# Modulation slabs multiplied two at a place, at every other place among the attention units

## The chip, the cores and the metric

One core of a Trainium2 chip runs the whole program. Its engines have instruction streams of their own and meet only at semaphores: PE (matrix multiply, with its weight loads as PEld), DVE (vector), ACT (activation), POOL and SP, which here issues the weight transfers. The metric is the device time of one execution in microseconds (us), lower is better.

## The reference, cut to what matters

Two blocks on 256 tokens of width 1024 in float32. The first is an attention of two kinds and a convolved feed-forward. The second has two layers; each layer needs six modulation vectors for the latents and six for the context, made of one conditioning vector each:

```python
c_act = jax.nn.silu(c)
cc_act = jax.nn.silu(c_ctx)
for l in range(DEPTH_2):
    ...
    mod_l = [m[:, None, :] for m in jnp.split(c_act @ ada_w[l] + ada_b[l], N_MOD, axis=-1)]
    mod_c = jnp.split(cc_act @ ada_w[l] + ada_b[l], N_MOD, axis=-1)
    ...
    h_l = modulate(xl, norm_mix_g[l], mod_l[0], mod_l[1])
    ...
    xl = xl + mod_l[5] * sq_relu_mlp(modulate(xl, norm_mlp_g[l], mod_l[3], mod_l[4]), w_mlp1[l], w_mlp2[l])
```

The matrices `ada_w` are 1024 x 6144 for each layer, 48 MB together. Their products have two rows each, and nothing needs them before the norm of the layer that they belong to.

## The kernel before, in words

All weights pass through a ring of four slots of 1 MB (`ring`, `SLOTS = 4`). SP issues slab after slab in the order in which they are used, and waits before each until the slab four places earlier in the order has been used up (`freed`). A modulation slab is 256 rows by 1024 columns of `ada_w`; there are 48, loaded by `load_mods` (the transfer is line 471). Multiplying one is `mod_rows_of`: eight float32 products of `cact` (two columns, padded to 32) with 256 columns, in four column groups of the array, into PSUM bank 4 or 5, which ends in a count on `mod_ready` (its rows in the profile are line 658). Four slabs in a row (n = 4d to 4d + 3) add up to one eighth of the twelve vectors of a layer; after the fourth, `copy_mods` on DVE (lines 2056 to 2066) transposes the bank and copies two columns of it to `mod_in`.

These slabs are put among the attention units, where PE's work comes in small pieces. There are three attention stages: that of block 1 (16 units, line 953 on, the first eight of kind A, the others of kind B), that of layer 0 of block 2 (32 units) and that of layer 1 (16 units). They get 12, 24 and 12 slabs. In layer 0 units alternate between long ones (latent queries, 512 keys) and short ones (context queries, 256 keys); in layer 1 all are long. Place u of the loop is what PE does in its turn u, in this order:

- the scores of unit u + 2 (`scores1`, line 916; `scores2`, line 1025), which need the exponentials of unit u done, since they use its PSUM banks
- the turn of unit u (`turn_weights`, line 929): PE transposes the weights of unit u. It waits for `a_ready` of unit u, except in units of kind A
- the outputs of unit u - 1 (`outputs1`, line 942; `outputs2`, line 1037)
- the modulation slab of this place, if it has one

DVE goes in its own order through turns of its own: the maximum of unit v (line 2331, in block 1 lines 2189 and 2193), the scaled output of unit v - 3 (`out2`, line 2352; `out1`, line 2219), the weights of unit v - 1 (`weights2`: reciprocal 2339, a small product 2342 and the combination 2346, which counts `a_ready`; `weights1`: 2208), and then `copy_mods` for the place v - 2. The output of unit v - 3 can be scaled only when PE's outputs of it are done, and the weights of unit v - 1 come behind it. In block 1 DVE also normalises two key heads in its turns 3 and 5 (`norm_head`, reciprocal at line 2171). ACT makes the exponentials (line 1619, 1464) and copies the turned weights out of PSUM (line 1473).

Which places have a slab is set by `spread(units, first, count)`: slab n of a stage goes to place n * units // count. With 12 slabs on 16 places and 24 on 32 this is every place except 3, 7, 11 and so on. After an attention stage of block 2 come the product with the narrow dt weights (line 765), the scaling of the outputs (line 2377) and the turns at line 845; `fill` (line 779) issues products whose result nobody uses.

Of the kernel before, what the change touches and what calls it, by code (L numbers as in the profile page):

```python
# [119 lines left out]
def two_blocks(nc, a, const, out):  # L120
    with ExitStack() as ctx:
# [41 lines left out]
        at = 9 * P  # L163
# [219 lines left out]
        at = 9 * P  # L383
# [36 lines left out]
        def spread(units, first, count):  # L420

            at = {}
            for n in range(count):
                at[n * units // count] = first + n
            return at

        mods_of = [spread(len(UNITS1), 0, EARLY), spread(len(units2(0)), EARLY, LATE + EARLY),
# [4 lines left out]
        def _(sp):  # L432
# [17 lines left out]
            mods = [0]  # L450
# [13 lines left out]
            def load_mods(n):  # L464

                for _ in range(n):
                    s = len(done) % SLOTS
                    freed(len(done))
                    l, j = divmod(mods[0], N_MOD // 2)
                    j, kk = divmod(j, 4)  # L470
                    sp.dma_start(slot(s, 2, D), of_layer("ada_w_2", l)[:, 2 * kk:2 * kk + 2, j * D:(j + 1) * D])\
                        .then_inc(slot_loaded[s], 16)
                    mods[0] += 1
                    booked((mod_ready, mods[0]))
# [40 lines left out]
            slabs(1, KT, 128, lambda j: w_in[:, :, 640:768], lambda j: 2 * j)  # L515
            sp.dma_start(K[:, 3 * P:], const[:, 3 * P:]).then_inc(tables_loaded, 16)
            wide(w_in, 768, 6)
            load_mods(len(mods_of[0]))
            wide(w_out, 0, 4)
            for j in range(FFT):  # L520
                up_slabs.append(len(done))
# [13 lines left out]
            for l in range(LAYERS):  # L535
                wi = of_layer("w_in_2", l)
                first_slab["q", l] = len(done)
                wide(wi, 0, 4)
                wide(wi, 1024, 4)
                wide(wi, 2048, 4, per=TT)  # L540
                wide(wi, C_GA, 4)
                load_mods(len(mods_of[1 + l]))
                slabs(1, KT, 64, lambda j: wi[:, :, C_DT:C_DT + 64], lambda j: TT * j)
                first_slab["attn_o", l] = len(done)
                wide(of_layer("w_attn_o_2", l), 0, 4)

                nz = len(y_chunks(l)) // 2
                per_group = 4 + nz
                after = [1, 2, 4, per_group]

                def group_parts(s, q, g):
                    half = slot(s, KT, P)
                    full = slot(s, KT, 256)
                    if q < 2:
                        return [(half, wi[:, :, bass.ds(g * GW + (C_X + q * P), P)])]
                    if q == 2:
                        return [(full[:, :, 0:P], wi[:, :, bass.ds(g * P + C_B, P)]),
                                (full[:, :, P:2 * P], wi[:, :, bass.ds(g * P + C_C, P)])]
                    return [(full, wi[:, :, bass.ds(g * GW + C_Z, GW)])]

                s0 = len(done)
                first_slab["ssd", l] = s0
                for q in range(4):
                    load(lambda s: group_parts(s, q, 0), after[q])
                with sp.Fori(1, GROUPS) as g:
                    for q in range(4):
                        s = (s0 + q) % SLOTS

                        sp.wait_ge(tile_ready, g * per_group + (total[0] + after[q] - per_group))
                        for dst, src in group_parts(s, q, g):  # L570
                            sp.dma_start(dst, src).then_inc(slot_loaded[s], 16)
                for g in range(1, GROUPS):
                    for q, n in enumerate(after):
                        booked((tile_ready, total[0] + per_group * g + n), 2 if q == 2 else 1)
                total[0] += per_group * GROUPS
                first_slab["gs", l] = len(done)
                for j in range(KT):
                    load(lambda s: [(slot(s, KT, P), wi[:, :, C_GS + j * P:C_GS + (j + 1) * P])], 1)
                    total[0] += 1
                first_slab["ssd_o", l] = len(done)  # L580
                wo = of_layer("w_ssd_o_2", l)
                slabs(KT, YT, P, lambda j: wo[:, :, bass.ds(j * P, P)], lambda j: j)
                wide(of_layer("w_out_2", l), 0, 4)
                w1, w2 = of_layer("w_mlp1_2", l), of_layer("w_mlp2_2", l)
                first_slab["mlp", l] = len(done)
                if l == 0:
                    for half in range(2):
                        wide(w1, half * HID // 2, HIDT // 4)
                        slabs(KT, YT, P, lambda j: w2[:, YT * half:YT * (half + 1), bass.ds(j * P, P)], lambda j: j)
                else:  # L590
                    wide(w1, 0, HIDT // 2)
                    for n in range(KT):
                        for half in range(2):
                            load(lambda s: [(slot(s, YT, P), w2[:, YT * half:YT * (half + 1), n * P:(n + 1) * P])], 1)
                        total[0] += 1
# [11 lines left out]
        def _(pe):  # L607
# [41 lines left out]
            def mod_rows_of(n):  # L649

                w = slot(weights(), 2, D).rearrange("p k (t g q) -> p k t g q", g=4, q=32)
                done, kk = divmod(n, 4)
                if kk == 0 and done > 1:
                    pe.wait_ge(mod_copied, done - 1)
                for k in range(2):
                    for g in range(4):
                        rows_of = PS[32 * g:32 * g + 32, 4 + done % 2, 0:256].rearrange("p (t q) -> p t q", q=32)
                        mm = pe.matmul(rows_of, cact[:, 2 * kk + k, :], w[:, k, :, g, :], start=(kk == 0 and k == 0),  # L658
                                       stop=(kk == 3 and k == 1))
                mm.then_inc(*c.made(mod_ready))  # L660
# [291 lines left out]
            for u in range(n_u + 1):  # L952
                if u + 2 < n_u:
                    scores1(u + 2)
                if u < n_u:
                    turn_weights(u, 4, prob[:, u % 2, 0:T] if UNITS1[u][0] == "A" else None)
                if u >= 1:
                    outputs1(u - 1)
                if u in mods_of[0]:
                    mod_rows_of(mods_of[0][u])  # L960
            c.skip(p_ready, 2)
            pe.wait_ge(*c.need(tok_scaled, LT))
            bank4[0] = 0
# [27 lines left out]
            for l in range(LAYERS):  # L991
# [24 lines left out]
                units = units2(l)  # L1016
# [25 lines left out]
                mods = mods_of[1 + l]  # L1042
# [3 lines left out]
                for u in range(n_u + 1):  # L1046
                    if u + 2 < n_u:
                        scores2(u + 2)
                    if u < n_u:
                        turn_weights(u, TT if units[u][1] < LT else LT)  # L1050
                    if u >= 1:
                        outputs2(u - 1)
                    if u in mods:
                        mod_rows_of(mods[u])
                c.skip(p_ready, 4)
                pe.wait_ge(*c.need(o_done))
                ring_begin(dve_freed)
# [909 lines left out]
        def _(dve):  # L1967
# [88 lines left out]
            def copy_mods(n):  # L2056

                done, kk = divmod(n, 4)
                dve.wait_ge(*c.need(mod_ready))
                if kk == 3:  # L2060
                    m0 = 8 * (done % (N_MOD // 8))
                    turned_rows = mod_rows[:, done % 2, :]
                    dve.transpose(turned_rows, PS[:, 4 + done % 2, 0:256]).then_inc(*c.made(mod_copied))
                    settle(mod_copied)
                    dve.tensor_copy(mod_in[:, m0:m0 + 8, :], turned_rows.rearrange("p (t q) -> p t q", q=32)[:, :, 0:2])\
                        .then_inc(*c.made(mod_read))
# [52 lines left out]
            for b in range(V_TURNS):  # L2119
                n = min(512, n_rows - 512 * b)  # L2120
# [112 lines left out]
            for u in range(n_u + 3):  # L2233
                if u < n_u:
                    max1(u)
                if u >= 3:
                    out1(u - 3)
                if u == n_u + 1:
                    scale_half(0)
                if 1 <= u <= n_u:  # L2240
                    weights1(u - 1)
                    settle()
                    settle(a_ready)
                if u in (3, 5):
                    norm_head(12 + (u - 3) // 2)
                if u - 2 in mods_of[0]:
                    copy_mods(mods_of[0][u - 2])
            settle(mod_read)
            c.skip(t_ready, 2)
            scale_half(1)  # L2250
# [44 lines left out]
            for l in range(LAYERS):  # L2295
# [60 lines left out]
                for u in range(n_u + 3):  # L2356
                    if u < n_u:
                        max2(u)
                    if u >= 3:
                        out2(u - 3)  # L2360
                    if 1 <= u <= n_u:
                        weights2(u - 1)
                    if u - 2 in mods:
                        copy_mods(mods[u - 2])
                c.skip(t_ready, 2)
                settle(mod_read)
                dve.wait_ge(*c.need(tok_rms))
# [532 lines left out]
```

## Time and profile before

| what | us |
|---|---|
| median of 3 runs | 2565.73 (2563.46 to 2565.87) |
| span of the profiled execution | 2566.1 |
| PE busy | 2489.1 (97%) |
| DVE, ACT, POOL busy | 1224.1, 1125.6, 1494.5 |

The span of the profile is 0.4 us above the median of the runs, and it carries no other time of its own, so what is worked out on the trace can be added to the median as it is. PE is busy for 97% of the span, the others for half of it or little more. A busy share is an average over stages, so it does not say what a change in one stage costs; for that the windows and timelines of the stage are read.

### The profile page before, as it was taken

Reading aid. Unit: us, or ns where it says so; the run is one execution under the profiler, and the core shown is the slowest. Engines: PE = TensorE matmul, PEld = TensorE weight load, DVE = VectorE, ACT = ScalarE, POOL = GpSimd, SP = SyncE. Lnnn points to the kernel's source line nnn. Section 1 sums busy time; section 2 is a strip of 40 time slices with the busy share of each in tenths; the row PEclk is TensorE's granted clock in tenths of the full one; section 3 lists DMA queues with packets and bytes.
Section 4 is the critical chain, followed back from the end, with each engine's and each line's share of the span. In section 5 each row is a group of like instructions: output and inputs, shape, how many; then the busy total and the mean of one; then the engine's idle time right before and its main releaser. Section 6 shows DMA issues by size and latency. Waiting matters only on the chain.

```text
span 2566.1 us, 39740 instructions
## 1 busy us (share of the span) xinstructions
PE 2489.1 (97%) x15548; PEld 2170.1 (85%) x15548; DVE 1224.1 (48%) x2583; ACT 1125.6 (44%) x2371; POOL 1494.5 (58%) x1318
## 2 busy tenths in 40 slices
PE   8999999999899999999999999999989999999999
PEld 7779997885688888888888888888859888889998
DVE  3545502236747888874243112121366888844210
ACT  2345533115526776774022002042364766654532
POOL 1019775870354554543975888864324666577976
PEclk9999999999999999999999999999999999999999
DMA  7566463237532222214322333332454233364564
GB/s 211 182 191 185 128 165 103 83 96 260 191 99 67 75 58 66 74 50 156 98 82 88 95 98 99 99 113 85 150 183 115 71 95 90 83 171 156 186 169 116
DMA packets 388969, 313.03 MB, mean 122 GB/s; under 512 B 12576, under 2 KB 374082, under 8 KB 387778
## 3 DMA queue, kind: packets, MB, share of 16 engines
q1 hardware_dynamic: 385874, 297.75, 39.2%
q10 hardware_dynamic: 2352, 12.59, 1.3%
q8 instruction: 109, 1.79, 0.3%
q0 software_dynamic: 576, 0.43, 0.2%
q14 instruction: 58, 0.48, 0.1%
HBM read 303.40 MB, written 7.34 MB: 121 GB/s over the span
## 4 chain that ended last, share of the span: by engine, by line
PE 73%; POOL 10%; DVE 7%; issue 5%; DMA 2%; ACT 2%; POOLq 1%; SPq 0%; DVEq 0%; ACTq 0%
PE PS L707 35%; PE PS L1109 10%; POOL rounded L2702 10%; PE PS L765 5%; PE PS L1116 4%; PE PS L730 2%; DVE mid_a L2445 2%; PE PS L1150 2%; PE PS L1237 2%; PE PS L658 2%; PE PS L1159 2%; PE PS L1037 1%; PE PS L929 1%; PE PS L1025 1%; PE PS L1171 1%
## 5 line engine op out<-in xcount | busy, mean ns | idle before, releaser
L2702 POOL TENSOR_TENSOR rounded<-ring,rounded 128x512 fp32r<-128x512 f32 (+1 forms) x872 | 1113.6, 1310 | 729.7 <-ACT rounded L1376 417.7
L707 PE MATMUL PS<-rounded 128*128 128x256 f32 (+1 forms) x6864 | 1135.4, 327 | 6.7 <-POOL rounded L2702 3.3
L707 PEld LDWEIGHTS PS<-rounded 128*128 128x128 f32 x6864 | 1016.6, 190 | 119.3 <-POOL rounded L2702 4.1
L2725 POOL TENSOR_TENSOR rounded<-ring,constants 128x512 fp32r<-128x512 f32 x216 | 229.3, 1092 | 248.2 <-PE PS L707 125.2
L1109 PE MATMUL PS<-rounded 128*128 128x512 f32 (+1 forms) x1536 | 343.5, 380 | 5.8 <-DVE mid_a L2445 5.1
L1109 PEld LDWEIGHTS PS<-rounded 128*128 128x128 f32 x1536 | 275.3, 188 | 61.2 <-DVE mid_a L2445 3.7
L1376 ACT ACTIVATE rounded<-ring 128x2048 fp32r<-128x2048 f32 (+1 forms) x99 | 180.0, 1822 | 136.6 <-DMA ring<-in_w_mlp_dram 55.1
L2445 DVE SCALAR_TENSOR_TENSOR mid_a<-PS,V,mid_a 128x510 f32<-128x510 f32 (+3 forms) x256 | 182.2, 714 | 25.5 <-ACT mid_a L1705 18.0
L1743 ACT ACTIVATE rounded<-constants,big 128x128 fp32r<-128x128 f32 x384 | 149.8, 390 | 0.0
L1743 ACT ACTIVATE rounded<-constants,mid_v 128x128 fp32r<-128x128 f32 x384 | 149.8, 390 | 0.0
L1116 PE MATMUL PS<-rounded 128*128 128x256 f32 x1152 | 147.8, 286 | 0.0
L1116 PEld LDWEIGHTS PS<-rounded 128*128 128x128 f32 x1152 | 142.6, 191 | 1.8
L1920 ACT ACTIVATE PS<-PS 128x512 f32<-128x512 f32 (+1 forms) x64 | 30.4, 475 | 251.7 <-DVE PS L2633 251.6
L2610 DVE SCALAR_TENSOR_TENSOR xT<-PS,mod,xT 128x256 f32<-128x256 f32 x40 | 17.9, 481 | 244.4 <-PE PS L707 244.4
L2633 DVE TENSOR_SCALAR PS<-PS 128x512 f32<-128x512 f32 (+1 forms) x64 | 36.1, 566 | 188.1 <-PE PS L707 177.8
L2482 DVE SCALAR_TENSOR_TENSOR big<-big,by_head 128x128 f32<-128x128 f32 x192 | 108.1, 621 | 18.9 <-POOL big L2803 18.6
L1659 ACT ACTIVATE rounded<-ring 128x1024 fp32r<-128x1024 f32 (+1 forms) x64 | 93.1, 1476 | 30.1 <-DMA ring<-in_w_in_dram 30.1
L765 PE MATMUL PS<-rounded 128*128 128x256 f32 x768 | 102.7, 290 | 0.0
L2318 DVE TENSOR_TENSOR edec<-PS,constants 128x256 f32<-128x256 f32 x32 | 13.6, 425 | 180.4 <-PE PS L1009 180.1
L765 PEld LDWEIGHTS PS<-rounded 128*128 128x128 f32 x768 | 96.3, 191 | 1.8
L2331 DVE TENSOR_REDUCE stat<-PS 128x2 f32<-128x1024 f32 (+1 forms) x48 | 50.0, 1045 | 81.0 <-PE PS L1025 80.8
L730 PE MATMUL PS<-rounded 128*128 128x256 f32 (+1 forms) x480 | 86.2, 339 | 1.4 <-DVE rounded L2623 0.9
(263 smaller groups left out, 3134.2 us busy)
## 6 DMA issues: line engine op xcount, KB each, us to landing
ring<-in_w_mlp_dram SPq DMA_DIRECT2D x64, 1024.0 KB, 5.5
ring<-in_w_in_dram SPq DMA_DIRECT2D x56, 1024.0 KB, 5.4
ring<-in_ada_w_dram SPq DMA_DIRECT2D x48, 1024.0 KB, 5.2
ring<-in_w_in_dram SPq DMA_DIRECT2D x81, 512.0 KB, 4.1
ring<-in_w_up_dram SPq DMA_DIRECT2D x44, 512.0 KB, 5.1
ring<-in_w_ssd_o_dram SPq DMA_DIRECT2D x16, 1024.0 KB, 5.9
ring<-in_w_out_dram SPq DMA_DIRECT2D x12, 1024.0 KB, 5.1
ring<-in_w_down_dram SPq DMA_DIRECT2D x16, 704.0 KB, 5.0
```

Of the source, the lines that this page charges most:

```text
L707: mm = pe.matmul(PS[:, b, 0:cols], w[:, k, m * P:(m + 1) * P], x(half * kt + k), start=(half == 0 and k == 0 and n_pass == 0), stop=(half ...
L730: mm = pe.matmul(PS[:, b, 0:cols], w[:, k, m % 2 * P:(m % 2 + 1) * P], x(k), start=(k == 0 and n_pass == 0), stop=(k == kt - 1 and n_pass ...
L765: mm = pe.matmul(PS[:, b, 0:width], x[:, k, t * P:(t + 1) * P], w[:, k, :], start=(k == 0 and n_pass == 0), stop=(k == KT - 1 and n_pass = ...
L1109: mm = pe.matmul(PS[:, b, 0:cols], w[:, k, m:m + P], x[:, k, 0:cols], start=(k == 0 and x is hs_hi and w is w_hi), stop=(k == KT - 1 and w ...
L1116: mm = pe.matmul(PS[:, b, t * GW:(t + 1) * GW], x[:, k, t0:t0 + P], w[:, k, :], start=(k == 0 and x is hs_hi and w is w_hi), stop=(k == KT ...
L1376: act.activation(view(R, at[n % len(at)], size), ring[:, slab % SLOTS, 0:size], ACT.Copy)\
L1659: act.activation(view(R, group_hi(s, q), words), ring[:, s, 0:words], ACT.Copy).then_inc(*c.made(round_ready))
L1743: act.activation(seg_parts[d][n][:, r * P:(r + 1) * P], mask, ACT.Copy, scale=dta_parts[n][:, t, h:h + 1]).then_inc(*c.made(seg_in))
L2445: ins = dve.scalar_tensor_tensor(out=cv[:, :, to], in0=u[:, :, fr], scalar=V[:, bass.ds(g * st + (cw + 32 * (d + 2) + off), 1)], in1=cv[:, ...
L2482: step(dve.scalar_tensor_tensor(out=m, in0=cb_lo[:, t, :], scalar=dt[:, t, g * GH + r:g * GH + r + 1], in1=m, op0=ALU.mult, op1=ALU.add))
L2702: ins = pool.tensor_tensor(lo[:, r], raw[:, r], hi[:, r], ALU.subtract)
L2725: ins = pool.tensor_tensor(hi[:, r], raw[:, r], ones[:, 0:1].broadcast_to([P, 512]), ALU.mult)
```

## The change

`spread` hands out two slabs at a time: for even n, slabs n and n + 1 both go to place n * units // count. Twelve slabs on 16 places now lie at places 0, 2, 5, 8, 10 and 13, two at each; 24 on 32 places lie at 0, 2, 5, 8, 10, 13, 16, 18, 21, 24, 26 and 29. PE multiplies the two behind each other, DVE takes both in the turn that belongs to the place. The same slabs are loaded in the same order.

```diff
         def spread(units, first, count):
 
             at = {}
-            for n in range(count):
-                at[n * units // count] = first + n
+            for n in range(0, count, 2):
+                at[n * units // count] = (first + n, first + n + 1)
             return at
...
-            load_mods(len(mods_of[0]))
+            load_mods(sum(map(len, mods_of[0].values())))
...
-                load_mods(len(mods_of[1 + l]))
+                load_mods(sum(map(len, mods_of[1 + l].values())))
...
-                if u in mods_of[0]:
-                    mod_rows_of(mods_of[0][u])
+                for n in mods_of[0].get(u, ()):
+                    mod_rows_of(n)
...
-                    if u in mods:
-                        mod_rows_of(mods[u])
+                    for n in mods.get(u, ()):
+                        mod_rows_of(n)
...
-                if u - 2 in mods_of[0]:
-                    copy_mods(mods_of[0][u - 2])
+                for n in mods_of[0].get(u - 2, ()):
+                    copy_mods(n)
...
-                    if u - 2 in mods:
-                        copy_mods(mods[u - 2])
+                    for n in mods.get(u - 2, ()):
+                        copy_mods(n)
```

## Rows read from the trace of the kernel before

**Rows 1.** Page, chain by engine; stages by window: us, busy PE, PEld, DVE, ACT, POOL, clock, DMA.

```profile
PE 73%; POOL 10%; DVE 7%; issue 5%; DMA 2%; ACT 2%; POOLq 1%; SPq 0%; DVEq 0%; ACTq 0%
...
96.00:147.00 51.00, 47.14 (x451) 32.21 (x449) 35.78 (x111) 31.22 (x91) 0.00 (x0) 0.97 0.77 257
585.00:682.00 97.00, 90.48 (x809) 54.00 (x809) 72.62 (x172) 61.66 (x225) 0.28 (x1) 1.00 0.83 281
1848.00:1907.00 59.00, 54.72 (x454) 32.75 (x454) 42.95 (x86) 36.21 (x111) 0.00 (x0) 1.00 0.74 233
```

**Rows 2.** Timeline of PE, layer 0, places 2 to 4: start, us, line, [idle before].

```profile
596.88 1.07 PE L658 MATMUL PS<-ring,cact 128*32 128x256 f32 x16
597.88 0.70 PE L1025 MATMUL PS<-big 64*128 64x256 f32 x4
598.51 0.44 PE L929 MATMUL PS<-constants,big 128*128 128x128 f32 x2
598.79 1.06 PE L1037 MATMUL PS<-mid_v,big 128*128 128x128 f32 x8
599.77 1.13 PE L1025 MATMUL PS<-big 64*128 64x512 f32 x4
601.40 0.66 PE L929 MATMUL PS<-constants,big 128*128 128x128 f32 x4 [0.50 <-DVE big L2346]
```

**Rows 3.** Timeline of DVE beside it.

```profile
596.03 1.23 DVE L2331 TENSOR_REDUCE stat<-PS 128x2 f32<-128x1024 f32 x1 [0.68 <-PE PS L1025]
597.17 0.34 DVE L2352 TENSOR_SCALAR mid_o<-PS,stat 128x128 f32<-128x128 f32 x1
...
597.88 0.48 DVE L2346 SCALAR_TENSOR_TENSOR big<-big,stat 128x256 f32<-128x256 f32 x1
...
599.88 0.35 DVE L2352 TENSOR_SCALAR mid_o<-PS,stat 128x128 f32<-128x128 f32 x1 [0.49 <-PE PS L1037]
...
600.34 0.22 DVE L2342 SCALAR_TENSOR_TENSOR stat<-stat,neg_lam 128x1 f32<-128x1 f32 x1
600.60 0.75 DVE L2346 SCALAR_TENSOR_TENSOR big<-big,stat 128x512 f32<-128x512 f32 x1
```

**Rows 4.** Waits of PE for DVE, layer 0, layer 1, block 1: total us, times, longest.

```profile
PE PS L929 <- DVE big L2346: 4.4, 9, 0.6
...
PE PS L929 <- DVE big L2346: 2.7, 5, 0.6
...
PE PS L929 <- DVE big L2208: 1.5, 4, 0.6
```

**Rows 5.** Timeline of PE, the last turns of layer 0 and of layer 1.

```profile
676.23 0.66 PE L929 MATMUL PS<-constants,big 128*128 128x128 f32 x4 [0.56 <-DVE big L2346]
...
678.70 0.44 PE L929 MATMUL PS<-constants,big 128*128 128x128 f32 x2 [0.36 <-DVE big L2346]
...
1903.69 0.66 PE L929 MATMUL PS<-constants,big 128*128 128x128 f32 x4 [0.63 <-DVE big L2346]
```

**Rows 6.** Timeline of block 1: two turns of kind A, two of kind B; DVE's reciprocal of a head.

```profile
109.95 0.66 PE L929 MATMUL PS<-constants,big 128*128 128x128 f32 x4
111.95 1.75 DVE L2171 RECIPROCAL big<-big 128x256 f32<-128x256 f32 x1
112.01 0.66 PE L929 MATMUL PS<-constants,big 128*128 128x128 f32 x4
...
121.19 0.66 PE L929 MATMUL PS<-constants,big 128*128 128x128 f32 x4
123.82 0.66 PE L929 MATMUL PS<-constants,big 128*128 128x128 f32 x4 [0.50 <-DVE big L2208]
```

**Rows 7.** Line 471, the transfers of the modulation slabs.

```profile
DMA to landing us min/median/max: 4.9/5.2/10.2
```

**Rows 8.** Windows after and at the end of layer 0's attention (columns as in rows 1).

```profile
676.00:682.00 6.00, 4.42 (x41) 3.30 (x41) 2.54 (x9) 2.69 (x12) 0.28 (x1) 1.00 1.07 350
690.00:694.00 4.00, 0.50 (x3) 0.51 (x4) 3.97 (x6) 0.00 (x0) 4.00 (x3) 0.56 0.80 262
```

## The prediction, made before the change was run

> **What bounds the kernel now.** I read the chain of work that ended last first, then windows over the three attention stages, then the timelines of PE and DVE inside them, and the waits of PE last. The chain runs on PE for 73% of the span, and in the three stages that the change touches PE is busy for 47.14 of 51, 90.48 of 97 and 54.72 of 59 us [rows 1]. So these stages go at PE's pace: what PE does there, and each wait of PE there, lengthens the kernel one for one. The reader is to see in the timeline of PE that pieces follow each other without a gap where a place has a slab, and that the one gap of 0.50 us stands in the turn that follows the place without one [rows 2]. The waits of PE for DVE's weights come to 4.4 us in 9 waits in layer 0, 2.7 in 5 in layer 1, 1.5 in 4 in block 1 [rows 4]: 8.6 us in all, and these are what a slab can hide.
>
> **Why a place without a slab (a bare place) costs.** Take the turn of unit 4 in layer 0. PE ends the outputs of unit 2 at about 599.77 and goes on to the scores of unit 6, which start then. Only after those outputs can DVE scale them (599.88), and the weights of unit 4 come behind that in DVE's order: a reciprocal, a small product at 600.34, the combination from 600.60 for 0.75 us; PE's turn starts at 601.40 [rows 2, 3]. That chain is 601.40 - 599.77 = 1.63 us long. PE has the scores of a long unit to put beside it, 1.13 us, so 1.63 - 1.13 = 0.50 us is left, which is the wait in the row. A slab between outputs and scores takes 597.88 - 596.88 = 1.00 us [rows 2], and 1.00 + 1.13 is more than 1.63: nothing is left. A second slab at the same place takes 1.00 us more and hides nothing, because nothing is left to hide. Nor does it put DVE ahead: three places with slabs in a row leave 0.5 us of slack each, and the wait after them is still the whole 0.50.
>
> For a short unit the last link is 0.48 us instead of 0.75 [rows 3], so the chain is 1.63 - 0.27 = 1.36 us, and the scores above it, of a short unit too, take 598.51 - 597.88 = 0.63 us [rows 2]: a bare place costs 0.73 us. Where the maximum of a long unit is in DVE's way, the scaling is later: at 597.17 it starts 0.29 us after PE went on at 596.88, behind a maximum that ran from 596.03, instead of 599.88 - 599.77 = 0.11 [rows 2, 3]. That is 0.18 us more, 0.90. No row of before shows a bare place ahead of a short unit, so these two are bounded. Unit 31 is short and waited 0.36 with a slab's 1.07 over it [rows 2, 5], so with only 0.63 over it the wait can't be under 0.36; and with nothing over it, it is the whole chain, 1.36 to 1.43. I take 0.73 and 0.90, which are nearest to the links of the chain as rows show them.
>
> **Layer 0** (32 units, pairs at 0, 2, 5, 8, 10, 13, 16, 18, 21, 24, 26, 29). Bare places were 8, and are 20. The turns behind them: 11 of long units (2, 4, 8, 10, 12, 16, 18, 20, 24, 26, 28) at 0.50, 5.5 us; short units 5, 13, 21, 29 at 0.73, 2.9 us; short units 7, 15, 23, behind a long unit's maximum, at 0.90, 2.7 us; and unit 31, ahead of which no scores are left, at 1.36 (before it had a slab's 1.00 over it and waited 0.36 [rows 5]), 1.4 us. Sum 12.5 us. Before it was 4.4 [rows 4]. Change +8.1 us.
>
> **Layer 1** (16 long units, pairs at 0, 2, 5, 8, 10, 13). Turns 2, 4, 5, 7, 8, 10, 12, 13 at 0.50 are 4.0 us, turn 15 has neither scores nor slab above it and waits the 1.63 (before 0.63 with a slab [rows 5]). Sum 5.6 against 2.7 [rows 4], change +2.9 us.
>
> **Block 1** (16 units, same places). In kind A PE does not wait for DVE's weights: turn 3 to turn 4, over the bare place 3, takes 112.01 - 109.95 = 2.06 us with no wait [rows 6]. Bare places in the first half are free, but for one: the reciprocal of a key head occupies DVE from 111.95 for 1.75 us [rows 6], the scaling of the outputs of unit 3 comes after it and after the maximum of unit 6, and PE's outputs of unit 4 need that. Place 4, now bare, no longer covers it: I work out 0.45 us. In kind B a bare place costs 0.50 (121.19 to 123.82 is 2.63 us with that wait in it [rows 6]); turns 8, 10, 12, 13 are 2.0 us, turn 15 without scores and slab 0.50 + 0.63 = 1.1. Sum 3.1 against 1.5 [rows 4]: +1.6, and with the 0.45, +2.1 us.
>
> **The rest of the edit.** PE's products, DVE's copies and ACT's work are the same in number and size: nothing. After a fourth slab DVE transposes and copies (some 0.6 us) in the turn of the pair, beside PE's bare place instead of beside a slab. In the order of DVE this lies between the weights of one unit and the maximum of the next; it can make a turn behind a bare place late by 0 to 0.4 us, at most once for each of the 12 copies (an estimate: DVE's own work for a unit of kind B fills the 2.6 us between turns behind a bare place, so little of the copy is covered). To see whether such things add up I laid the durations of the rows end to end in the order of the three engines, each step at the later of its own engine and of what it needs. For before this puts the turn of unit 31 of layer 0 77.1 us behind that of unit 4; in the trace it is 678.70 - 601.40 = 77.3 [rows 2, 5]. For the new places it gives +8.1, +3.1 and +2.4 us, 13.5 in all, against 8.1 + 2.9 + 2.1 = 13.1 by hand. I take 13.3.
>
> **Transfers.** The order of the slabs is kept. SP issues a slab when the slab four before it has been used, so a pair is replaced by the pair after next, at least five places later: by the laid-out durations its second slab is wanted 13.3 us after its slot came free. Landing takes 5.2 us in the median and 10.2 at most [rows 7]; two behind each other at the median are 10.4. That is under 13.3, so loads cost nothing; were this cover gone, PE would wait for the second slab of a pair. The slabs of attn_o and w_out behind the modulation slabs are issued at the same place or a place sooner, and no wait of PE behind the stages is for them.
>
> **What the stage's end covers.** Behind each stage PE waits for DVE's scaling, which starts when the last unit is done; nothing there was early. So none of the 13.3 us is given back.
>
> **Forecast.** 2565.7 + 13.3 = 2579.0 us.
>
> **Rivals.**
> *Faster: the pair banks its lead.* If DVE and ACT could use the second slab's 1.00 us to get ahead, a pair would cover the two bare places behind it (slack of 0.5 + 1.0 against 2 x 0.50) and all the waits would go: 2565.7 - 8.6 = 2557.1. It decides from the point where the weights of a unit are ready a whole place before their turn. For it: the buffers are two deep. Against it: the weights of unit u stand in DVE's order behind the scaled output of unit u - 2, which PE makes one place before; and slack did not save up over three slab places [rows 2]. Chance 0.03.
> *No change: half of it is banked.* If the bare place next to a pair were free and only the second in a row paid, there would be 4 + 8 + 4 = 16 paying places of about 0.5 us, 8 us against 8.6: 2565.1. The same row speaks against it. Chance 0.04.
> *Much slower: the second slab of a pair is late.* If in layer 0, where demand is highest (281 GB/s [rows 1]), both transfers of a pair took the longest landing, one behind the other, 20.4 us would go by from the issue of the first, which is 1.0 us ahead of the second; the second is wanted 14.7 us after its slot came free, by the laid-out durations. That is 20.4 - 1.0 - 14.7 = 4.7 us late, for each of the 10 pairs that are reloaded: 2579.0 + 47 = 2626. Against it: the median is half of that, and line 658 waits for nothing in the trace. Chance 0.03.
> *Slower: the clock falls.* In a window of 4 us in which PE is busy for 0.50 the granted clock is 0.56, that is near 1.2 GHz instead of 2.4; in the window 676 to 682, where it is busy for 4.42 of 6.00, it kept 1.00 [rows 8]. Should short waits in a row bring it down, the work of the second bare place, 2.06 us, would double at each of the 16 pairs of bare places: +33, 2612. Chance 0.04. The Trainium skill (TensorE: Matmul & The Clock Gate, section "A second HAM failure mode: psum-queue depth-cycling") says that a kernel whose PE pauses briefly and often between groups of products can swing between half and full clock; that speaks against this change, and by it the time would be nearer to this rival. The trace does not agree with it so far: the last six microseconds of layer 0's attention are idle for 1.58 us in short waits and show 1.00 [rows 8].
>
> **How the numbers follow.** The forecast has 0.86. Its own range, low end: long turns at 0.40 and short ones at 0.36, the least that rows allow [rows 5], no copy in the way and no 0.45 give 11 x 0.40 + 7 x 0.36 + 1.4 - 4.4 = +3.9, 8 x 0.40 + 1.6 - 2.7 = +2.1 and 4 x 0.40 + 1.1 - 1.5 = +1.2, 7.2 in all, 2573. High end: long turns at 0.63, the longest wait behind a long unit [rows 5], short ones at 0.90 give +10.2, +3.9 and +2.6, and the copies in half of their places 6 x 0.4 = 2.4, 19.1 in all, 2585. The range 2573 to 2585 leaves 0.14 to the rivals and needs no widening. About 0.2% (5.1 us) is what a measurement of this kernel can tell from no change. Faster by more than that: the first rival, 0.03. Within: the second, 0.04. Slower: 0.93.
>
> **What would show it.** The windows of the three stages should grow from 51, 97 and 59 us to about 53, 105 and 62; the waits of PE's turn for DVE from 4.4, 2.7 and 1.5 us to about 12.5, 5.6 and 3.1, in about 20, 9 and 5 waits; slabs should still take 1.00 us each and wait for nothing; outside the stages nothing should move by more than 0.5 us. A wait in front of line 658 would mean the third rival, a granted clock under 1.00 inside layer 0 the fourth, waits of 0.50 behind only every other bare place the second. The prediction would be wrong if PE's waits stayed near 8.6 us, or if something behind a stage had been waiting for its slabs all along.

## Result: 9 to 11 us slower

| | before | changed |
|---|---|---|
| median of 6 runs each | 2565.57 us (2563.46 to 2567.08) | 2575.02 us (2571.47 to 2580.92) |
| ratio to before, 95% interval | | 1.0038 [1.0028, 1.0048] |
| the profiled execution | 2565.9 us | 2580.92 us, its span 2579.1 us |
| predicted | | 2579.0 us (2573 to 2585) |

The change costs 9.45 us. Timed once more beside the experiments it cost 11.1 us (ratio 1.0046 [1.0032, 1.0060]); that is e10 below. Forecast were 13.3 us: inside the range, and 20 to 40% more than the two measurements.

The profile after. First the chain by engine and the three stages in windows (us, busy PE, PEld, DVE, ACT, POOL, granted clock, DMA share, GB/s), which answer to [rows 1]; the windows were chosen for this trace, from the stage's first work to just behind its last:

```profile
PE 68%; POOL 10%; DVE 8%; issue 5%; DMA 1%; ACT 1%; POOLq 1%; SPq 0%; DVEq 0%; ACTq 0%
...
96.00:150.00 54.00, 48.58 (x456) 34.76 (x452) 35.17 (x110) 31.37 (x94) 0.00 (x0) 0.93 0.74 254
588.00:692.00 104.00, 89.52 (x809) 55.23 (x809) 72.41 (x172) 61.64 (x225) 0.26 (x1) 1.00 0.74 263
1859.00:1920.00 61.00, 54.18 (x454) 33.38 (x454) 42.70 (x85) 35.87 (x111) 0.00 (x0) 1.00 0.66 227
```

The stages are 3, 7 and 2 us longer, with the same records on PE (456 for 451, 809, 454), and PE is busy in them for slightly less than before in two of the three. What was added is idle time of PE. Whose it is, the waits of PE say (engine, line waited at, releaser: us, times, longest), for layer 0, layer 1 and the two places of block 1, as in [rows 4]:

```profile
PE PS L929 <- DVE big L2346: 12.1, 19, 1.3
...
PE PS L929 <- DVE big L2346: 5.6, 9, 1.6
...
PE PS L929 <- DVE big L2208: 3.1, 5, 1.1
...
PE PS L942 <- DVE mid_o L2219: 0.9, 2, 0.6
```

Forecast were 12.5 us in about 20 waits, 5.6 in 9, 3.1 in 5, and 0.45 at the outputs of unit 4 of block 1. The timeline of PE shows each kind at its place, beside the pair of slabs (start, duration, line, [idle before]):

```profile
600.62 1.93 PE L658 MATMUL PS<-ring,cact 128*32 128x256 f32 x32
602.48 0.70 PE L1025 MATMUL PS<-big 64*128 64x256 f32 x4
603.12 0.44 PE L929 MATMUL PS<-constants,big 128*128 128x128 f32 x2
603.39 1.06 PE L1037 MATMUL PS<-mid_v,big 128*128 128x128 f32 x8
604.38 1.13 PE L1025 MATMUL PS<-big 64*128 64x512 f32 x4
606.01 0.66 PE L929 MATMUL PS<-constants,big 128*128 128x128 f32 x4 [0.50 <-DVE big L2346]
606.50 0.61 PE L1037 MATMUL PS<-mid_v,big 128*128 128x128 f32 x4
607.04 0.70 PE L1025 MATMUL PS<-big 64*128 64x256 f32 x4
608.40 0.44 PE L929 MATMUL PS<-constants,big 128*128 128x128 f32 x2 [0.66 <-DVE big L2346]
...
615.18 0.44 PE L929 MATMUL PS<-constants,big 128*128 128x128 f32 x2 [0.86 <-DVE big L2346]
...
688.72 0.44 PE L929 MATMUL PS<-constants,big 128*128 128x128 f32 x2 [1.29 <-DVE big L2346]
```

Behind the pair at place 2 the turn comes without a wait. Then come the two bare places 3 and 4: behind the first the long unit's turn waits 0.50 us (forecast 0.50), behind the second the short one's 0.66 (0.73). A short turn behind a long unit's maximum waits 0.86 (0.90), unit 31 waits 1.29 (1.36). And the first row holds what was missed: the pair takes 602.48 - 600.62 = 1.86 us, not twice the 1.00 of [rows 2].

To compare stages below I take the time from the first turn (line 929) to the product with the dt weights (line 765) in the layers, and to the first turn at line 845 in block 1. Before: 91.39 us in layer 0, 53.78 in layer 1 and 46.88 in block 1; this last has a stretch with a granted clock of 0.58 in it (see e4), so for block 1 the measure of before is e2, which has its placement and no such stretch inside the stage.

### The profile page after: what moved, and what is told of

Read it like the earlier page. It is cut to its first block, busy times and chain, and to the rows that moved or that the text cites. A ratio compares the mean times of both kernels' runs of the same rounds, so it can differ in the third digit from the quotient of the medians.

```text
span 2579.1 us, 39731 instructions
## 1 busy us (share of the span) xinstructions
PE 2490.9 (97%) x15548; PEld 2176.5 (84%) x15548; DVE 1218.1 (47%) x2583; ACT 1125.6 (44%) x2371; POOL 1494.4 (58%) x1318
## 4 chain that ended last, share of the span: by engine, by line
PE 68%; POOL 10%; DVE 8%; issue 5%; DMA 1%; ACT 1%; POOLq 1%; SPq 0%; DVEq 0%; ACTq 0%
PE PS L707 32%; PE PS L1109 10%; POOL rounded L2702 10%; PE PS L765 4%; PE PS L1116 4%; PE PS L730 2%; DVE mid_a L2445 2%; PE PS L1150 2%; PE PS L1237 2%; PE PS L658 2%; PE PS L1159 2%; PE PS L1037 1%; PE PS L929 1%; PE PS L1171 1%; DVE mid_v L2499 1%
```

## Experiments

Each experiment is compared with runs of the kernel before made beside it. Their medians are 2564.67 us for e1 to e4, 2565.30 for e5 to e8 and 2564.91 for e9 and e10.

**e1 and e2: one stage's share at a time.** `spread` gets the number of slabs a place as an argument; e1 pairs them in block 1 alone, e2 in the two layers alone.

```diff
-        def spread(units, first, count):
+        def spread(units, first, count, step):
...
-            for n in range(0, count, 2):
-                at[n * units // count] = (first + n, first + n + 1)
+            for n in range(0, count, step):
+                at[n * units // count] = tuple(range(first + n, first + n + step))
```

e1 calls it with 2, 1, 1 for the three stages, e2 with 1, 2, 2.

> Two slabs at a place in block 1 only; layers 0 and 1 keep one slab at a place, as before. Theory (each bare place costs the wait that a slab hid, a pair of slabs in one piece costs 1.86 us instead of 2 x 1.00): waits of PE's turn for DVE's weights in block 1 go from 1.5 to about 3.1 us, one wait of 0.35 to 0.45 for the scaled output, six pairs give back 6 x 0.14 = 0.8 us: +1.3 us against before, with the granted clock at 1.00 to the end of the stage. Clock theory: the 1.07 us wait in front of the last turn, which was 0.17 before, lets the clock fall to half at 146 us as in the profile of the changed kernel; then the end of the stage and the first product of w_out take 2 to 3 us more, +3 to +5 against before. Rival (nothing in block 1 matters since behind it is slack): 0.

> Two slabs at a place in layers 0 and 1 only; block 1 as before. Theory: layer 0 +6.4 to +6.7 us, layer 1 +2.1 to +2.3 us as the sum of waits (12.1 against 4.4, 5.6 against 2.7) less 0.14 us for each of 18 pairs: +8.5 to +9 us against before, and no spread between runs beyond that of before, since the clock is at 1.00 in both stages. If the clock fall behind block 1 is what spread the runs of the changed kernel, this one has none of it. Rival (the layers' waits are covered by slack behind the stages): under +4.

e1: 2565.83 us, ratio 1.0010 [1.0001, 1.0019], +1.2 us. e2: 2574.99 us, ratio 1.0040 [1.0026, 1.0054], +10.3 us. The layers' share is somewhat above the 8.5 to 9 expected. Together 11.5, against 9.45 and 11.1 for the whole change: the stages add up, and no paying back of one in another is seen. The stages themselves: block 1 47.00 us in e1 against 45.45 in e2, layer 0 91.38 in e1 against 98.17 in e2, layer 1 53.77 against 56.12. That is +1.55, +6.8 and +2.35, 10.7 us.

**e3: is it the work or the cover?** At each bare place of layers 0 and 1 the changed kernel also multiplies one idle product, of about 0.5 us, into the modulation bank that is not in use; its result is never read.

```diff
+            def idle_products(next_slab, k):
...
+                for _ in range(k):
+                    pe.matmul(PS[:, 4 + done % 2, 256:512], ones, K[:, 0:SEQ], start=True, stop=True)
...
+                    if u not in mods and u < n_u:
+                        idle_products(done_mods, 1)
```

> The changed kernel, with one product whose result nobody uses (128 x 256, about 0.5 us of PE) put at each of the 30 bare places of layers 0 and 1. Theory (PE waits there anyway for the chain outputs, scaled output, weights, turn): the product takes the place of the wait; the waits of the turn for DVE fall from 12.1 and 5.6 us by about 0.5 each, and the time stays that of the changed kernel within 2 us. Rival (PE's own work is what the places cost): 30 x 0.5 = +15 us against the changed kernel, about 2590.

The two layers last 98.13 and 56.13 us, as without the 30 products (98.15 and 56.12 in e10); the kernel takes 2577.27 us, ratio 1.0060 [1.0044, 1.0076], in four runs. That is 12.6 us over before, where the changed kernel was 9.45 and 11.1 over it and the rival wanted some 25. Waits and timeline of PE in layer 0 (line 670 is the product; PE's other lines have moved by 10, DVE's by 13):

```profile
597.53 0.60 PE L670 MATMUL PS<-constants 128*128 128x256 f32 x2
598.05 1.13 PE L1035 MATMUL PS<-big 64*128 64x512 f32 x4
599.25 0.66 PE L939 MATMUL PS<-constants,big 128*128 128x128 f32 x4
...
601.64 0.44 PE L939 MATMUL PS<-constants,big 128*128 128x128 f32 x2 [0.23 <-DVE big L2359]
```

```profile
PE PS L939 <- DVE big L2359: 3.2, 9, 0.9
```

The long turn has no wait left, the short one 0.23 instead of 0.66: the waits fall from 12.1 to 3.2 us and the stage keeps its length. A bare place has about half a microsecond free, and the turn's time is set by DVE's chain, not by PE's work. A pair's second slab lies outside that gap, behind the turn that has nothing left to hide.

**e4: does the clock fall at the end of block 1 because of the change?** In the profiled execution of the changed kernel the granted clock drops there. Windows as above:

```profile
144.00:148.00 4.00, 3.08 (x20) 2.98 (x21) 1.70 (x7) 2.08 (x6) 0.00 (x0) 0.77 1.10 361
148.00:152.00 4.00, 2.99 (x15) 2.59 (x15) 1.34 (x4) 2.69 (x8) 0.00 (x0) 0.50 0.14 43
```

0.50 is 1.2 GHz. At the beginning of this stretch PE had waited 1.07 us for the turn of unit 15 (144.34). e4 is the changed kernel with two idle products in each of the last two places of block 1:

```diff
+                if n_u - 2 <= u < n_u:
+                    idle_products(EARLY, 2)
```

> The changed kernel, with two products whose result nobody uses at each of the last two bare places of block 1 (14 and 15), about 1.0 us each, where PE waited 1.07 and 0.57 us. Theory (the idle end of block 1's attention lets the granted clock fall to half, from about 146 to 156 us, in some executions): the clock stays at 1.00 there, the stretch from the last turn to the second product group of w_out is 2 to 3 us shorter than in the profile of the changed kernel, and the runs spread less, at about 2573. Rival (the clock falls for the window's own phase whatever PE does there): it falls here too, and the time is that of the changed kernel.

e4: 2575.73 us (about 2573 expected), ratio 1.0044 [1.0031, 1.0056], clock 1.00 in both windows, block 1 47.11 us. But the changed kernel itself, profiled once more (e10), has 1.00 there too, at 47.01 us, and so has e1; and e2, whose block 1 is that of before, fell (so did e5 below). Windows of e2 and then of e10:

```profile
144.00:148.00 4.00, 2.20 (x17) 1.97 (x17) 1.75 (x6) 2.65 (x9) 0.00 (x0) 0.90 0.58 185
148.00:152.00 4.00, 4.00 (x17) 3.58 (x16) 0.00 (x0) 1.75 (x4) 0.00 (x0) 0.67 0.02 4
```

```profile
144.00:148.00 4.00, 2.81 (x24) 2.46 (x23) 1.54 (x5) 2.40 (x7) 0.00 (x0) 1.00 0.88 288
148.00:152.00 4.00, 2.82 (x17) 2.62 (x18) 1.05 (x3) 2.96 (x8) 0.00 (x0) 1.00 0.03 6
```

So this fall goes with the execution and not with the placement, as far as one profile each can tell; it does not explain the 10 us. The start of block 1 varies in the same way (granted clock from 100 to 104: 0.58 before, 0.78 in the changed kernel, 1.00 in e1, e2, e4 and e10). The profiled pair of executions differs by 13.0 us of span, which looks like the forecast of 13.3, but by luck: against e10 the first profile of the changed kernel loses some 3.5 us between the last turn of block 1 and the second group of products with the weights behind it, where its clock fell, and not every execution has this. What makes an execution fall stays open.

**e5: four slabs at every fourth slab's place.** The same as e1 with 4, 4, 4.

> Four slabs at a place, at every fourth slab's place (0, 5, 10 on 16 places; 0, 5, 10, 16, 21, 26 on 32). Theory by the laid-out durations (each place without a slab costs its wait, a piece of k slabs costs 0.14 + 0.86 k us): block 1 +3.2, layer 0 +10.4, layer 1 +4.6, +18 us against before, if the four slabs are in the ring when PE comes to them. Four transfers of 1 MB have five places, some 13 to 15 us, from the slot coming free to use: at 2.7 us each behind each other and 5.2 to land they just fit. Transfer rival: PE waits in front of the slabs (line 658), 1 to 5 us at each of the nine groups that are reloaded, +10 to +40 more. Rival (a bare place costs nothing if another bare one precedes it): waits stay near those of pairs, +12.

2590.07 us, ratio 1.0098 [1.0082, 1.0113], +24.8 where 18 were expected. Timeline and waits of PE in layer 0, and the landing of the slabs' transfers (line 471, us):

```profile
599.53 2.80 PE L658 MATMUL PS<-ring,cact 128*32 128x256 f32 x48
603.60 1.07 PE L658 MATMUL PS<-ring,cact 128*32 128x256 f32 x16 [1.27 <-DMA ring<-in_ada_w_dram]
...
617.06 3.66 PE L658 MATMUL PS<-ring,cact 128*32 128x256 f32 x64
620.65 0.70 PE L1025 MATMUL PS<-big 64*128 64x512 f32 x2
```

```profile
PE PS L929 <- DVE big L2346: 16.5, 25, 1.6
```

```profile
DMA to landing us min/median/max: 5.0/7.7/11.4
```

The bare places in a row all pay: nothing is banked by four either. PE now waits for a slab too, once, 1.27 us at the first group of layer 0. So the transfers' rival exists with four slabs, though far smaller than its 10 us; with two, PE waits for no transfer at line 658, and the landing takes 6.0 us in the median (5.2 in [rows 7]). The stages are longer by 5.4 us (expected 3.2), 12.7 (10.4) and 4.85 (4.6). In block 1 some 2.5 us of this are slow products at its end, where the granted clock was 0.63 and then 0.50; in layer 0 it is the wait for the slab and a price of each wait that is worked out further down; the rest of the 24.8 stays open. Four slabs in one piece take 620.65 - 617.06 = 3.59 us. With 1.00 for one and 1.86 for two, a piece of k slabs takes 0.14 + 0.86 k us.

**e6: parts of slabs, so that no place is bare where that costs.** From the kernel before: the eight products of a slab may be split over places. Layer 0's places get 7 and 4 products by turns, most of layer 1's get 4 each; what is over lies at the last places, which have little else above the turn. Block 1 keeps bare places in kind A, where they are free.

```diff
+        PLACED = [[8, 0, 8, 0, 16, 0, 0, 8, 8, 4, 8, 4, 8, 12, 12, 0], [7, 4] * 14 + [7, 15, 12, 4], [8] + [4] * 12 + [16, 16, 8]]
...
+            def mod_products(first, last):
...
+                for m in range(first, last):
+                    n, j = divmod(m, 8)
```

> From the kernel before: the same slabs, cut into their eight products and dealt out over nearly all places: layer 0 seven and four products in turn, then 7, 15, 12, 4 at the last places; layer 1 eight, twelve times four, then 16, 16, 8; block 1 8, 0, 8, 0, 16, 0, 0, 8, 8, 4, 8, 4, 8, 12, 12, 0. Theory: four products (0.14 + 4 x 0.107 = 0.57 us) are enough to hide the wait of 0.50 at a place ahead of a long unit, twelve or more hide the 1.36 to 1.63 of the last ones: block 1 -1.7, layer 0 -3.4, layer 1 -2.8, -7.9 us against before, waits of the turn for DVE near 3, 0 and 0.5 us. Rival (the number of pieces counts, since each breaks PE's stream): no gain or up to +2.

2559.54 us, ratio 0.9978 [0.9969, 0.9987]: 5.8 us faster than before, 2 less than expected. PE's turn waits nowhere for the weights. Timeline of PE in layer 0 (line 664 are the slabs' products):

```profile
590.49 1.06 PE L664 MATMUL PS<-ring,cact 128*32 128x256 f32 x14
591.49 0.70 PE L1032 MATMUL PS<-big 64*128 64x256 f32 x4
...
593.38 0.64 PE L664 MATMUL PS<-ring,cact 128*32 128x256 f32 x8
593.95 1.13 PE L1032 MATMUL PS<-big 64*128 64x512 f32 x4
```

Four products take 0.57 us, which is 0.14 + 0.86 / 2. Seven take 1.00, as much as eight: time goes by begun groups of four. Sixteen pieces of the layer (fifteen with 7 products, one with 15, which takes 1.86 like 16) are one product short of a full group and pay about 0.1 us each, 1.7 in all. Layer 0 is 89.04 us, 2.35 less than before where 3.4 were expected. The trace adds up: the waits for weights are gone (4.4 us, and 9 x 0.07 that they cost besides, see below), and the slabs take 26.9 us instead of 24.2. A layout with full groups only was not run. Layer 1 is 3.05 us shorter (2.8 expected).

**e7 and e8: DVE's order.** The chain outputs, scaled output, weights, turn exists because DVE works in program order and has the scaled output of unit u - 3 ahead of the weights of unit u - 1. The weights don't need it. e7 is the kernel before, e8 the changed one, with the two exchanged, in block 1 and in both layers:

```diff
+                    if 1 <= u <= n_u:
+                        weights2(u - 1)
...
-                    if 1 <= u <= n_u:
-                        weights2(u - 1)
```

(the moved lines now stand ahead of the scaled output instead of behind it; the same with `weights1` in block 1.)

> From the kernel before, one slab at a place: DVE makes the weights of unit v - 1 before it scales the output of unit v - 3, instead of after. Theory (the chain outputs, scaled output, weights, turn is what a bare place leaves open, and it hangs on DVE's order, not on DVE's speed): with the weights first nothing of PE's previous place stands in the chain; waits of the turn for DVE fall from 4.4, 2.7 and 1.5 us to about 0, 0 and 1, and the time by about 8: -8 us against before. New wait: the outputs of unit u - 1 need the scaled output of unit u - 2, which now comes later; the laid-out durations see little of it. Rival (DVE as a whole is too slow for a bare place): waits stay, time within 2 us of before.

> The same order of DVE with two slabs at a place, as in the changed kernel. Theory: bare places then cost little, and pairs differ from singles by +3 us only, not by +10: about -5 us against before, block 1 -0.2, layer 0 -1.5, layer 1 -3.3. Rival (pairs cost for another reason than this chain, for example their transfers): +10 against e7_weights_first as between the two kernels.

e7: 2557.70 us, ratio 0.9970 [0.9958, 0.9982], 7.6 us faster (8 expected). Timeline of PE and DVE over a bare place of layer 0:

```profile
596.28 1.06 PE L1037 MATMUL PS<-mid_v,big 128*128 128x128 f32 x8
...
597.25 0.75 DVE L2346 SCALAR_TENSOR_TENSOR big<-big,stat 128x512 f32<-128x512 f32 x1
597.27 1.13 PE L1025 MATMUL PS<-big 64*128 64x512 f32 x4
597.92 0.34 DVE L2352 TENSOR_SCALAR mid_o<-PS,stat 128x128 f32<-128x128 f32 x1
598.33 0.66 PE L929 MATMUL PS<-constants,big 128*128 128x128 f32 x4
```

The outputs end when the scores begin, at 597.27. The combination of the weights starts at 597.25, without waiting for them, and the turn follows the scores at 598.33 with no wait. No wait for weights is left in layer 0.

e8: 2562.98 us, ratio 0.9990 [0.9981, 0.9999], 2.3 us faster than before and 5.3 slower than e7. With this order pairs still cost something, less than the 10 us that they cost in the old one, and more than the 3 expected. Timeline and waits in layer 0:

```profile
600.13 1.23 DVE L2331 TENSOR_REDUCE stat<-PS 128x2 f32<-128x1024 f32 x1 [0.24 <-PE PS L1025]
...
601.72 0.48 DVE L2346 SCALAR_TENSOR_TENSOR big<-big,stat 128x256 f32<-128x256 f32 x1
...
602.26 0.44 PE L929 MATMUL PS<-constants,big 128*128 128x128 f32 x2 [0.51 <-DVE big L2346]
```

```profile
PE PS L929 <- DVE big L2346: 4.4, 8, 0.7
```

The eight waits are at the turns of short units. There the maximum of a long unit (1.23 us from 600.13) holds DVE, the short unit's weights follow it, and the turn comes when they are done. It is the next link of the same kind: the bare place shows the step of DVE that now stands in front of the weights.

**e9: the better of both.** Weights first, single slabs in block 1 and layer 0, pairs in layer 1, where all units are long and pairs cost nothing once the weights go first (50.69 us in e8, 51.32 in e7).

> Weights first in DVE's order (as e7_weights_first), one slab at a place in block 1 and layer 0, two at a place in layer 1. Theory: layer 1 then needs nothing to hide (its waits are near 0 with either placement) and gains 0.14 us for each of 6 pairs, measured as 50.69 against 51.32 us in the two kernels before; so -0.6 us against e7_weights_first, about -8.2 against before. That is under what the runs can tell apart; the stage's length in the trace is to show it: 50.7 us in layer 1, 86.3 in layer 0. Rival (pairs cost something in layer 1 that e8_weights_first_pairs hid): layer 1 at 51.3 or more.

2554.57 us, ratio 0.9958 [0.9945, 0.9972]: 10.3 us faster than before, the lowest median here (8.2 expected). Its interval and that of e7 overlap; the gain over e7 that the trace shows is that of layer 1, 0.64 us: layer 0 takes 86.34 us, as in e7, layer 1 50.68 (51.32 in e7). Six fewer pieces are 0.8 us by the formula of e5.

**e10: the changed kernel again**, beside e9 and for its clock.

> The changed kernel as it is, once more, beside before on this chip. Theory: layer 0 98.1 us and layer 1 56.1 us from first turn to the dt product, as in the first profile, and +10 us against before (1.5 + 6.7 + 2.3 = 10.5 by stages). If the granted clock at the end of block 1 is 1.00 this time, its fall in the first profile (0.50 from 147 to 156 us) is not part of the change. Clock theory: it falls again, and the median stays at +10 or more with a spread to +15.

2575.98 us, ratio 1.0046 [1.0032, 1.0060]. Layer 0 98.15 us, layer 1 56.12, block 1 47.01 with the clock at 1.00.

## Why the prediction was right, and where its size was not

**PE sets the pace of these stages, and a bare place costs what the chain outputs, scaled output, weights, turn leaves uncovered.** Right, and shown from three sides: e3 adds PE work in the gap for nothing; e7 takes the scaled output out of the chain and the waits go, but for 0.9 us in three waits in block 1 and layer 1; e6 covers every place that costs and they go too.

**The single waits.** Right: 0.50 as forecast, 0.66 for 0.73, 0.86 for 0.90, 1.29 for 1.36. In block 1 PE waited 0.35 us for the scaled output of place 4, where 0.45 was worked out from the reciprocal of a key head:

```profile
114.52 1.10 PE L942 MATMUL PS<-mid_v,big 128*128 128x64 f32 x8 [0.35 <-DVE mid_o L2219]
```

The sum of the waits grew by 7.7 + 2.9 + 1.6 + 0.35 = 12.6 us; forecast 13.1 by hand, 13.3 taken. The low end's 0.40 for a long unit's turn was called the least that rows allow, but stands in none of the rows it names; in the two layers no long turn waited less than 0.50, before or after, and in block 1 the added ones waited 0.45 and more.

**"A second slab at the same place takes 1.00 us more."** This step failed. It takes 0.86. The 1.00 of [rows 2] is start to start of a piece with one slab and includes 0.14 us that a piece costs once, however many slabs are in it. The change makes 24 pieces of 48, so 24 x 0.14 = 3.4 us are given back, and of the 13.3 us 9.9 would be left. That this lies between the two measurements, 9.45 and 11.1, is partly luck, since the waits came to 12.6 and a second term is missing (see the sum by stage). The prediction put PE's products under "nothing", because their number and size stay; but their grouping changes, and that has a price. No row of before shows two slabs in a piece, but pieces of another kind hint at it: a turn of two products takes 0.44 us, one of four 0.66 [rows 2], less than twice as much. What the 0.14 us is, is argued only: these products use the array as 128 x 32, their neighbours as 128 x 128 or 64 x 128. The Trainium skill (TensorEngine Tiling (Array Packing), section "Tiling Modes") says that changing the tiling mode drains TensorE. The pieces of one, two and four slabs agree with such a cost, 0.14 us for going in and out together; no run tells it from another fixed cost of a piece.

**Sum by stage.** With waits and pieces the stages should grow by 7.7 - 1.7 = 6.0, 2.9 - 0.8 = 2.1 and 1.95 - 0.8 = 1.1 us, 9.2 in all. They grew by 6.8, 2.35 and 1.55 (at full clock), 10.7 in all. Most of the 1.5 us between lie in a second term that the prediction left out: a wait costs more than the idle time that the profile shows for it. Scores of a long unit with no wait behind them (two rows of the changed kernel, start of the scores and of the turn)

```profile
611.53 1.13 PE L1025 MATMUL PS<-big 64*128 64x512 f32 x4
612.59 0.66 PE L929 MATMUL PS<-constants,big 128*128 128x128 f32 x4
```

take 612.59 - 611.53 = 1.06 us from start to start, since the next piece begins before the end that the profile gives them. With a wait behind them (604.38 above) they take 606.01 - 604.38 - 0.50 = 1.13. The prediction set 1.13 against the chain and 0.50 as the price of a bare place; start to start the price is 0.57. The change adds 10, 4 and 2 waits, 16 x 0.07 = 1.1 us, so 12.6 + 1.1 - 3.4 = 10.3 of the 10.7. The same term closes layer 0 in e7: 4.4 us of waits and 9 x 0.07 are 5.05, and the stage is 91.39 - 86.34 = 5.05 shorter. DVE's copies after a fourth slab, which the prediction let cost 0 to 0.4 us at most twelve times, hardly show: all the eight waits of layer 1 before its last are 0.50, and in layer 0 one long turn has 0.68 instead.

**Transfers cost nothing.** Right with two slabs a place. With four, in e5, PE waits once for a slab, 1.27 us.

**"So none of the 13.3 us is given back" behind the stages.** Right as far as can be told: e1 and e2 add up to the whole, and the stages' 10.7 us lie between the measured 9.45 and 11.1.

**Nothing outside the stages moves by more than 0.5 us.** Not to be seen in single profiles: from the end of block 1's stage to the start of layer 0's they have 443.2 us (before), 445.5 (changed), 441.7 (e10, the same kernel) and 438.7 (e1), so executions of one kernel differ by more than 0.5 us there.

**The rivals.** *The pair banks its lead*: refuted in the changed kernel and again with four slabs in e5; in both layers and in kind B every turn behind a bare place waits. *Half of it is banked*: the turns behind the first and the second of two bare places both wait (0.50 and 0.66 above). *The second slab is late*: not with two. *The clock falls*: in layers 0 and 1 the granted clock was 1.00 with 19 and 9 short waits of 0.5 to 1.6 us, so the swing between half and full clock that the Trainium skill (TensorE: Matmul & The Clock Gate, section "A second HAM failure mode: psum-queue depth-cycling") tells of, for brief and frequent pauses, is not seen here. The fall at the end of block 1 is in one of the two profiles of the changed kernel, and in e2 without pairs there.

## What to carry to other kernels

Filler work on the critical engine is worth what it covers at its own place. Here a lead could not be saved, since each turn stood in DVE's order behind an output made one place before; two fillers in one gap covered no more than one. First look at why the gap is there: the order in which a second engine takes two steps that don't depend on each other was worth at least about as much (7.6 us in e7) as the best placement of the fillers tried (5.8 us in e6; the intervals overlap), for a far smaller edit. The two together were not run. And cost a regrouping by the piece, start to start, not only by the instruction.

## What the runs showed of the hardware

A run of 128 x 32 products between others costs 0.14 us once, and 0.43 us for every begun group of four (4 products 0.57, 7 and 8 products 1.00, 15 and 16 products 1.86, 32 products 3.59 us). A wait of PE costs 0.07 us besides the idle time that the profile shows: the scores of a long unit take 1.06 us start to start when the next piece follows at once, and 1.13 up to the idle time when it doesn't. A product of about 0.5 us at each of thirty bare places left both stages as long as without, within 0.02 us. Waits of 0.5 to 1.3 us, 19 in 98 us, left the granted clock at 1.00; whether it falls at the end of block 1 differed between two executions of the changed kernel, by some 3.5 us.
